# Two transformer blocks on one core: low parts on GpSimd, transfers moved back, km ahead of the angles, dummy matmuls ahead of the first turn

## The reference

```python
mod = c @ w_ada[l] + b_ada[l]
shift_m, scale_m, gate_m, shift_f, scale_f, gate_f = jnp.split(mod, 6, axis=-1)
h = modulate(rms_norm(x, g_pre_mix[l]), shift_m, scale_m)
proj = h @ w_in[l]
q_a, k_a, v_a, q_m, k_m, v_m, o_m, i_m, f_m, g_a, g_m = jnp.split(proj, split_points, axis=-1)
q_a = rope(q_a.reshape(B, S, N_Q_HEADS, HEAD_DIM), positions)
...
qk_m = jax.nn.silu(causal_depthwise_conv(jnp.concatenate([q_m, k_m], axis=-1), conv_w[l], conv_b[l]))
i_pre = i_m + b_if[l][:MLSTM_HEADS]
f_pre = f_m + b_if[l][MLSTM_HEADS:]
...
y_m = (jax.nn.sigmoid(o_m.astype(jnp.float32)) * head_layer_norm(h_m, mlstm_norm_w[l])).astype(x.dtype)
```

## Time and profile before

| what | value |
|---|---|
| median of 3 runs | 820.08 us (815.45 to 822.45) |
| the profiled execution, device time | 822.01 us |
| its span in the profile | 820.2 us |
| TensorE busy | 767.2 us, 94% of the span |
| DVE busy | 638.1 us, 78% |
| ACT busy | 393.8 us, 48% |
| GpSimd busy | 29.0 us, 4% |
| DMA | 173.67 MB, mean 212 GB/s |

### The profile page before, as it was taken

One profiled execution on the slowest core, in us unless ns is written; L12 is line 12 of the kernel. 1 busy time (PEld: TensorE's weight loads), 2 busy tenths in 40 slices (PEclk: granted clock), 3 DMA queues, 4 the chain that ended last, 5 costly groups with the idle time before them and its releaser, 6 DMA issues.

```text
span 820.2 us, 15828 instructions
## 1 busy us (share of the span) xinstructions
PE 767.2 (94%) x6598; PEld 702.9 (86%) x6598; DVE 638.1 (78%) x838; ACT 393.8 (48%) x554; POOL 29.0 (4%) x44
## 2 busy tenths in 40 slices
PE   0999998998998999999999999989998999999996
PEld 0888998997887999999878987889878999999874
DVE  5759988888986887867987899886599678556457
ACT  3356753575464445344354894533125544454440
POOL 0110000000001000000001000050010000000000
PEclk9999999999999999999999999999999999999999
DMA  9795586682656999989992643600363679565621
GB/s 357 255 343 200 163 258 230 208 281 83 218 188 191 343 318 309 321 279 318 345 348 86 222 147 116 200 3 3 105 226 109 207 243 340 177 196 190 196 97 52
DMA packets 96021, 173.67 MB, mean 212 GB/s; under 512 B 7768, under 2 KB 55231, under 8 KB 95951
## 3 DMA queue, kind: packets, MB, share of 16 engines
q1 hardware_dynamic: 93630, 166.62, 60.9%
q0 software_dynamic: 1872, 5.86, 2.4%
q10 hardware_dynamic: 448, 0.19, 0.1%
HBM read 171.60 MB, written 1.05 MB: 210 GB/s over the span
## 4 chain that ended last, share of the span: by engine, by line
PE 69%; DVE 18%; DMA 6%; ACT 4%; issue 3%; DVEq 0%; POOL 0%; ACTq 0%; POOLq 0%
PE bank L2087 12%; PE bank L2088 12%; PE bank L2089 12%; PE bank L2352 5%; PE bank L2354 4%; PE bank L2353 4%; DVE wlo L459 3%; PE bank L2062 2%; PE bank L2064 2%; PE bank L2063 2%; DMA raw<-in_w_in 2%; DMA cc<-in_c 2%; PE bank L2514 1%; DVE acc L486 1%; DMA raw<-in_w_ada 1%
## 5 line engine op out<-in xcount | busy, mean ns | idle before, releaser
L650 ACT ACTIVATE whi<-raw 128x1024 fp32r<-128x1024 f32 (+1 forms) x212 | 220.9, 1053 | 225.4 <-PE bank L2089 99.2
L459 DVE TENSOR_TENSOR wlo<-raw,whi 128x1024 fp32r<-128x1024 f32 (+1 forms) x212 | 254.2, 1214 | 87.0 <-ACT whi L650 83.3
L2087 PE MATMUL bank<-hh,whi 128*128 128x256 f32 x1016 | 286.3, 282 | 10.7 <-DVE wlo L459 7.4
L2088 PE MATMUL bank<-hl,whi 128*128 128x256 f32 x1016 | 283.8, 279 | 0.0
L2089 PE MATMUL bank<-hh,wlo 128*128 128x256 f32 x1016 | 283.7, 279 | 0.0
L2087 PEld LDWEIGHTS bank<-hh,whi 128*128 128x128 f32 x1016 | 193.1, 190 | 14.8 <-issue 10.2
L2088 PEld LDWEIGHTS bank<-hl,whi 128*128 128x128 f32 x1016 | 192.6, 190 | 0.4 <-issue 0.2
L2089 PEld LDWEIGHTS bank<-hh,wlo 128*128 128x128 f32 x1016 | 192.5, 189 | 0.0
L486 DVE SCALAR_TENSOR_TENSOR acc<-raw,cc,acc 128x1024 f32<-128x1024 f32 x56 | 71.7, 1280 | 5.5 <-DMA raw<-in_w_ada 3.3
L2352 PE MATMUL bank<-whi,ffh 128*128 128x512 f32 x168 | 65.6, 391 | 0.9 <-DVE wlo L459 0.9
L2353 PE MATMUL bank<-wlo,ffh 128*128 128x512 f32 x168 | 65.4, 389 | 0.0
(11 more groups left out here) (453 smaller groups left out, 1081.2 us busy)
## 6 DMA issues: line engine op xcount, KB each, us to landing
raw<-in_w_ada SPq DMA_DIRECT2D x96, 512.0 KB, 5.2
raw<-in_w_in SPq DMA_DIRECT2D x54, 512.0 KB, 4.6
raw<-in_w_ffn_in SPq DMA_DIRECT2D x88, 256.0 KB, 3.9
raw<-in_w_ffn_gate SPq DMA_DIRECT2D x44, 256.0 KB, 4.3
raw<-in_w_ffn_up SPq DMA_DIRECT2D x44, 256.0 KB, 5.8
raw<-in_w_ffn_down SPq DMA_DIRECT2D x22, 512.0 KB, 5.3
raw<-in_w_ffn_out SPq DMA_DIRECT2D x22, 512.0 KB, 4.3
raw<-in_w_out SPq DMA_DIRECT2D x16, 512.0 KB, 4.3
```

The source lines that it names most:

```text
L459: eng.tensor_tensor(lo[:, 0:nk * width], raw[:, b % RAW, 0:nk * width], hi[:, 0:nk * width].bitcast(fp), ALU.subtract)\
L650: act.activation(weight_place(g)[0][:, 0:nk * width], raw[:, b % RAW, 0:nk * width], ACT.Copy)\
L2087: mm(o, wh[:, k, c], xh[:, kk_, :], start=first, stop=False)
L2088: mm(o, wh[:, k, c], xl[:, kk_, :], start=False, stop=False)
```

## The change

- GpSimd makes the low parts of o_if's blocks 2 to 5, in front of its spreads; DVE keeps 0, 1, 6 and 7. Those who wait for a block (`ready`) wait for the engine that made it. ACT splits blocks 4 and 5 between the halves of `scale_h(0)`.
- The 18 small transfers go from blocks 28 to 36 (two each) to blocks 33 to 38 (three each). GpSimd's four later spreads wait for the first conv copy of qm.
- On DVE the i and f biases come first, then km's first low part, the `osig` products, km's other three, and then the angles. ACT's sine moves behind the copy of qm's columns, ahead of vm's high parts.
- On TensorE 52 dummy matmuls come ahead of the first turn, 40 instead of 32 ahead of `part(1)`, and the turn of the second block's vectors goes behind vm.

```diff
-        ready = [("dve", b + 1) for b in range(len(order))]
+        ready, made_by = [], {"dve": 0, "pool": 0}
+        for o in order:
+            who = "pool" if o[0] == "o_if" and 2 <= o[1] < 6 else "dve"
+            made_by[who] += 1
+            ready.append((who, made_by[who]))
...
-                if 28 <= b < 37:
-                    for n in (2 * (b - 28), 2 * (b - 28) + 1):
+                if 33 <= b < 39:
+                    for n in range(3 * (b - 33), 3 * (b - 33) + 3):
                         small_transfer(n)
...
+            prepare_on(pool, "pool", "o_if")
...
             pool.wait_ge(sem("spreads"), 3 * 16)
+            pool.wait_ge(sem("conv_raw"), 1)
             spread(bcs[:, 1, :], A["sg_ln_g_2"][0], sem("spreads"))
...
-            scale_h(0)
-            split("o_if", slice(4, 8))
+            scale_h(0, lambda: split("o_if", slice(4, 6)))
+            split("o_if", slice(6, 8))
             split("qm")
...
             split("km")
-
-            act.wait_ge(sem("angles"), 1)
-            act.activation(cossin, rsc[:, 1], ACT.Sin).then_inc(sem("cossin_ready"), 1)
...
                 if nxt:
+                    act.wait_ge(sem("angles"), 1)
+                    act.activation(cossin, rsc[:, 1], ACT.Sin).then_inc(sem("cossin_ready"), 1)
                     split(nxt)
...
             prepare("qm")
 
+            dve.wait_ge(sem("osig_ready"), 1)
+            dve.wait_ge(sem("spreads"), 3 * 16)
+            for m in range(MT):
+                TT(st[:, 240 + 8 * m:248 + 8 * m], bank[4 + m][:, 252:260], bsm[:, 0:8], ALU.add)\
+                    .then_inc(sem("if_ready"), 1)
+
+            prepare("km", slice(0, 1))
+            dve.wait_ge(sem(f"pair{place['o_if'][0] % 2}_free"), place["o_if"][0] // 2 + 1)
+            for m in range(MT):
+                step(TT(osig[:, m, :], osig[:, m, :], bcs[:, 0, :], ALU.mult))
+            prepare("km", slice(1, None))
             dve.wait_ge(sem("small_in"), 32)
...
             turn_vectors(0, bank[2], n1)
+            run_on(26, 3)
             turn_h(0, lambda m: xn[:, m * D:(m + 1) * D], "xn_ready", 0)
             part(0)
-            run_on(16, 3)
+            run_on(20, 3)
             part(1)
...
             last.then_inc(sem("if_turned"), 1)
+            tokens_out("vm", 512, modulated)
             pe.wait_ge(sem("vectors2_in"), 16 * (len(ROWS2) + 2))
             turn_vectors(1, bank[4], n2)
-            tokens_out("vm", 512, modulated)
             features_out("g0", four, modulated)
```

More of the change, by code:

```diff
@@ L651, in split, with scale_h @@
                        .then_inc(sem("hi_ready"), 1)
-            def scale_h(u):
+            def scale_h(u, between=None):
                 g = gain[:, u, :]
@@ L670, in scale_h @@
                            .then_inc(sem("hh_ready"), 1)
+                    if between and half == 0:
+                        between()
             def branch_gates(n):
@@ L1214, in _ @@
             TS(red, ang, SIN_MAX, -SIN_MAX, ALU.min, ALU.max).then_inc(sem("angles"), 1)
[L1217 to L1226, removed]
             for t in range(8):
```

## The result

The changed kernel took **826.53 us** (median of 5 runs, 825.38 to 827.78), the kernel before 820.08 (now 5 runs, with the same median as the first 3): a ratio of 1.0082, 95% interval 1.0045 to 1.0119. One execution of a later run, e5, fell in a slower state of the chip (880.8 us at a mean granted clock of 0.84) and is left out of its numbers. The profiled execution took 826.53 us too (span 824.7), while that of before lay 1.9 us above its median.

What follows compares the result with a forecast made beforehand. TensorE (69% of the span) bounds the kernel where it waits or runs at the lower clock. At g0, 72.15 + 11.11 + 0.35 + 1.5 = 85.1 against 86.97, 1.9 us earlier, carried through to 818.2 us; range 812.8 to 821.8.

Steps and rivals of the forecast that it cites:

- Step 1: At the head, the new dummies let part(1) start at 29.15 and DVE's step come at 30.47, not 33.62: 3.15 us won.
- Step 2: At the head, GpSimd's o_if low parts lengthen DVE's second low part by 0.7 us; DVE's step still 2.45 us earlier.
- Step 3: Later spreads and constants win 0 alone and cost 0, but keep qm's third block from losing 2 us of the head.
- part 2: The change's item giving GpSimd o_if's low parts 2 to 5, priced at 0.7 us on DVE's second low part.
- Step 4: km's low parts ahead of the angles: km's 3.05 us wait and 1.5 of clock go; TensorE stands 3.5 at vm.
- Steps 5 and 6: Behind the new vm wait the lower clock loses 1.5 us; the second vector turn adds 0.35 us ahead of g0.
- the slower one: Rival at the head: the lower clock returns before the turn, 1.5 us later than before, 821.6 us; chance 0.15.

Runs made afterwards that it cites:

- e5: Changed kernel with GpSimd's four later spreads not waiting for the conv copy; 823.9 us, ratio 1.0052.
- e3: Kernel before with only the new order of angles and km's low parts on DVE and ACT; 822.4 us, ratio 1.0015.
- e14: Kernel before with only the small transfers moved to blocks 33 to 38; 826.7 us, ratio 1.0091.
- e18: Kernel before with the small transfers two blocks earlier, at blocks 26 to 34; 820.7 us, ratio 1.0004.
- e1: Kernel before with only the new dummies, 52 ahead of the first turn and 40 ahead of part(1); 820.9 us, ratio 0.9999.
- e7: Changed kernel with the dummies of before, none ahead of the first turn and 32 ahead of part(1); 824.2 us, ratio 1.0060.
- e16: e12 with the 52 dummies ahead of the turn and the 40 ahead of part(1); 819.6 us, ratio 0.9982.
- e8: Changed kernel with GpSimd's first low part waiting until both gains are made; 825.7 us, ratio 1.0076.
- e9: Changed kernel with DVE's and ACT's order of the kernel before; 822.3 us, ratio 1.0015.
- e13: Changed kernel with the small transfers at blocks 28 to 36 again, two each; 824.3 us, ratio 1.0037.
- e2: Kernel before with only GpSimd's four low parts of o_if; 818.3 us, ratio 0.9962.
- e11: Kernel before with GpSimd's low parts and the small transfers at blocks 33 to 38; 826.5 us, ratio 1.0069.
- e12: Changed kernel with angles between km's first and second low part, spreads not waiting, transfers at blocks 28 to 36, dummies of before; 817.7 us, ratio 0.9964.
- e15: e12 with the small transfers put back to blocks 33 to 38; 823.4 us, ratio 1.0046.
- e17: Changed kernel measured again, unchanged, against the kernel before; 824.9 us, ratio 1.0057.
- e6: Changed kernel with the angles between km's first and its other low parts; 822.0 us, ratio 1.0026.

## Why the prediction was wrong, step by step

*Step 1, dummies, 3.15 us won: failed.* In the profile of after the turn was fast and modT came at 30.81, just as written. But the 33.62 that I subtracted from is one of several values that the head of before has by itself. Three other executions with the same code of the head (e3, e14, e18) had the modT step at 30.30, 30.30 and 30.55, and the first o_if at 33.53 to 33.77. The 3.15 us are a difference between executions, and the runs price the dummies at nothing that they can resolve (e1, e7, e16). The profiles show why. Of the eleven with the 52 dummies five have `part(1)` early, at 29.1 to 29.9 us (after, e8, e9, e13, e16), and six late, at 31.2 to 34.0; of the nine without them four are early, at 29.0 to 29.3, and five late, at 32.6 to 33.0. In nine of the eleven the turn took 2.57 to 3.68 us instead of 2.13: the clock had not held up to it. This is the step that turned the sign: without the 2.45 us of head that it and step 2 gave, the forecast at g0 is +0.55 instead of -1.9.

*Step 2, GpSimd's price of 0.7 on the second low part: mis-sized, and at the wrong instruction.* The second low part was untouched (1.31 for two) and two gain steps paid 1.04 and 1.05 us. (Five versions without the 52 dummies, e2, e7, e11, e12 and e15, did show that low part held: 2.40 us for the two.) Against an early head of before, the heads with GpSimd's products start o_if 1.9 to 2.6 us later (35.67 in e2, 36.12 in after, against 33.53 to 33.77), and TensorE waits about 3 us there. I had drawn on a rule of the Trainium skill (GPSIMD Engine Reference, Key points), which names DVE instructions in a two-port mode or with two SBUF inputs. I used the second half only, which covers L1159; the steps with one SBUF tensor that were held here (L1153 1.21 for 0.17, L1226 1.80 for 0.20) could only come under the first. It gives no price; these rows do. What I did not count at all is the gain: slots freed early, and with them e2's 0.38%.

*Step 3, transfers at no cost: right at most in the changed kernel's own order.* I named them the cover for part 2. No run shows them as a cover: e2 and e12 do better without, and in the three pairs of runs with the angles ahead of km's last low parts they cost 0.8 to 1.1% (e14 against before, e15 against e12, e11 against e2). In the changed kernel itself the constants were issued at 47.33 and landed at 56.3, 6 us before the angles. Elsewhere the cost was the later issue (8.7 us later in e14) or issue and queue together (7.7 later and 5.2 longer on the way in e11 than in e2).

*Step 4, wait moved from km to vm: right, 3.5 us forecast, 5.34 measured.* km had no wait. vm came at 76.88 instead of 72.15. Of these 4.7 us, 3.2 come with km's fourth low part, ready at 62.56 instead of 59.35 (o_if 1.7 later, and 1.5 of clock behind the wait ahead of it), and 1.6 are the memset on the angle step L1226. I had seen the spreads go behind the conv copy, but not that the memset goes with them, onto the path of DVE.

*In one sum.* At g0 the profile stood 4.8 us behind the forecast (89.92 against 85.1): 1.7 from o_if coming late behind the held gain steps, 1.5 from the clock behind it, 1.6 from the angle step beside the memset. Another 1.5 came between g0 and the end, which I had taken as nothing. The last 1.9 are the distance of the profile of before from its own median, which after's profile does not have. Together 8.2 of the 8.3 us between 818.2 and 826.5. It is the account of one pair of profiles.

*Steps 5 and 6: right.* The clock was 0.50 behind vm's wait, and the vector turn at 89.57 stands ahead of g0.

*The rest.* From g0 on I carried the difference through unchanged; in the profiles it grew from +2.95 to +4.4 at 268, where TensorE waited 3.46 us for a low part instead of 2.70. What it grows by was not tried. *The rivals:* the slower one, the clock back down before the turn, had the sign. In the profile of after it was not the cause, since the turn ran at full clock, but it is what e1 and eight other profiles with the dummies show. Its price of 1.5 us was a quarter of the loss.

Settled by the runs: GpSimd alone wins 0.38%; the order alone wins nothing, since it moves the wait from km to vm, and beside GpSimd's slots the wait that it is aimed at is gone anyway (e2); the dummies win nothing; the late transfers lose unless the angles are last, and the angles last hold conv and vm. Open is how much of the loss each of hold, clock and transfers has in the changed kernel, since each alone is under the 2 us that these runs resolve.

## What to carry to other kernels

Before a stall in one profile is counted as a gain, look at a second execution: the head, with TensorE's clock in it, ended up to 3.3 us apart between executions of the same code. When a wait is removed by reordering a busy engine, add up all that now stands ahead of its next customer, with what other engines' instructions do to it. And for each transfer that is moved back, find its first reader and put both the issue and the time to landing against it.

## What the runs showed of the hardware

- GpSimd's reading or writing of SBUF held DVE's small steps until its instruction ended: 4 columns took 1.06 to 1.25 us instead of 0.16 or 0.17 (after, e2, e17), 64 columns 1.80 instead of 0.20 and a conv tile 1.69 instead of 0.41 (e6), both beside a memset of about 1.0 us. The steps L1171 at 36.49, which read a bank of PSUM, lay inside a product of GpSimd (36.20 to 38.99) and took 0.99 us for two, as without it.
- GpSimd's 128x520 products took 1.26 to 1.49 us each; four in a row, partly beside DVE's `hl`, took 5.96 (e8).
- The granted clock stayed 1.00 through waits of TensorE of 2.85 (e1), 2.93 (e13) and 3.00 us (e2). In e9 (3.44) and e16 (3.29) it stayed through the wait and fell 0.4 us after TensorE had started again. In after it fell ahead of the wait of 2.80 us, and 2.0 us into the one of 5.34 ahead of vm; in e13 it stayed 1.00 through 5.3 us of the same wait. The Trainium skill (TensorE: Matmul & The Clock Gate, What's actually happening) has the lower clock as the default that activity releases; these rows agree, and the length of the wait alone does not decide it.
